# Scaling a gathered row in two halves, so that the adding engine can begin on the first

## The chip, the cores and the metric

The kernel runs on one core of one Trainium2 chip. The metric is device time in microseconds (us), the median of the runs shown. Five engines work side by side and meet only at semaphores: TensorE (PE in the profile, with its weight loads as PEld), VectorE (DVE), ScalarE (ACT), GpSimd (POOL) and SyncE (SP). Transfers run on 16 DMA engines.

## The reference, cut to what matters

The program is one layer of a transformer over 1024 tokens of width 1024. Its last part, and the longest, is PEER: each token looks up 128 of 16384 single-neuron experts (8 heads, 16 each) and adds their value rows, weighted.

```python
def block(args):
    xb, eb, gb = args
    ub = u[eb]
    act = jax.nn.gelu(jnp.einsum('thkd,td->thk', ub, xb).astype(jnp.float32),
                      approximate=False)
    w = (gb * act).astype(xb.dtype)
    return jnp.einsum('thk,thkd->td', w, v_emb[eb])
```

For a block of 128 tokens, u[eb] and v_emb[eb] are 128 gathered rows for each token. The kernel keeps u and v side by side in one table `uv`, so one gathered row holds 2048 numbers.

## The kernel before, in words

The phases ahead (norm, gated linear attention, most of the stick-breaking attention, memory attention for the first half of the tokens) end some 740 us into the span. Then `expert_phase` runs to the end. Its main loop goes over 8 blocks of 128 tokens, in each over 8 heads, in each over 16 chosen experts: 1024 steps, numbered R. A step treats one "row": for each of the 128 tokens (one to a partition) the 8 KB of its R-th expert, 1 MB in all.

Rows pass through a ring of 8 buffers (`Ring`: `early_rows` and `rows`, four each). The way of row R:

1. POOL waits until row R-8 has been used (`row_used`) and issues the indirect gather (line 2029).
2. DVE waits for it to land and takes the product of its u half with the tokens, summed (line 3045, `dots`).
3. ACT waits for `dots`, applies Gelu to the 128x1 result (line 3223), multiplies by the gate (line 3225), and scales the v half, 128x1024, in place by this weight (line 3231), which counts up `row_scaled`. The weight is an operand with one number for each partition.
4. PE waits for `row_scaled` and adds the v half to the block's sum `expert_acc` in PSUM with 8 transposing products of 128x128 (line 3539). The eighth counts up `row_used`, which frees the buffer.

The last three rows (LAST) end differently: the first of them is scaled as the others and added by DVE (line 2694) with the last two, which DVE scales itself.

Around these steps each engine has side work, put into the stream at fixed values of R by the tables `Later` and `Dense` through the functions `later(R)` and `densely(R)`: the rest of the layer for the second half of the tokens (attention, memory attention, query and key products), the choice of experts for coming groups, and from R about 524 a dense treatment of the 16 most wanted experts' tiles for the last three blocks, whose rows are then not gathered (their index lies out of bounds, in the list `expert_sk`). Every engine takes its stream in order. On ACT the side work lies between line 3231 of one row and line 3223 of the next; twice in a group of 16 rows ACT changes its function table.

Of the kernel before, what the change touches and what calls it, by code (L numbers as in the profile page):

```python
# [12 lines left out]
ACT = mybir.ActivationFunctionType  # L13
# [8 lines left out]
HALF = 512  # L22
# [43 lines left out]
class Core:  # L66
# [53 lines left out]
    def sb(self, name, shape, dt=F32, ctx=None, side=None):  # L120
        return (ctx or self.ctx).enter_context(self.nc.sbuf_tensor(name, shape, dt, side=side))
# [2209 lines left out]
def expert_phase(co, choice, ring, scores, rstd, uv, gf, g_final, out, k_t, v_m, z_b, mix_b, w_out, w_mq, w_mo, w_pq,  # L2331
# [3 lines left out]
    nc = co.nc  # L2335
# [48 lines left out]
    with ExitStack() as cx:  # L2384
# [8 lines left out]
        wt = sb("wt", [P, 2, 2, TOPK])  # L2393
# [95 lines left out]
        def rows_of(g):  # L2489

            b, h = divmod(g - PH * dense.FIRST, PH)
            if b < 0:
                return places_of(g)
            cols = slice(TOPK * h, TOPK * (h + 1))
            return skip_index[:, b, cols], skip_gates[:, b, cols]

        def position(g):

            return g if g < PH * HB else dense.turn_of[g]
# [165 lines left out]
        def _(dve):  # L2665
# [19 lines left out]
            def row_sum(R):  # L2685

                first = NB * BLOCK - LAST
                v = rows[R % ROWS][:, D:E]
                before = rows[first % ROWS][:, D:E]
                last = R == NB * BLOCK - 1  # L2690
                r = R % TOPK
                dve.wait_ge(row_scaled, first + 1)
                dve.wait_ge(last_weighed, R - first)
                return nc.vector.scalar_tensor_tensor(hb[:, :] if last else before, v, wt[:, (PH - 1) % 2, 1, r:r + 1], before,
                                                      ALU.mult, ALU.add)
# [379 lines left out]
        def _(act):  # L3075
            link = Chain(act, act_done)

            def scores_in(n):
                g = dense.group.get(n, n)
                dst = s_in[:, n % 2, :, :]  # L3080
                if at.EARLY // 2 <= g < PH:
                    act.wait_ge(a_kept, 2 * (g - at.EARLY // 2 + 1))
                if g >= PH * HB:
                    act.wait_ge(side_kept, 4 * (g % PH + 1))
                dst = dst.rearrange("p c n -> p (c n)")
                nc.scalar.activation(dst, group_scores(g), ACT.Copy).then_inc(s_ready, 1)

            def sum_squares(b):
                act.wait_ge(acc_turned, b + 1)
                nc.scalar.activation(hb[:, :], accs[b % 2][:, :], ACT.Square, accum_out=small2[:, 0:1]).then_inc(summed, 1)  # L3090

            def finish(b):
                act.preload_act_table_set(LN_EXP)
                act.wait_ge(var_ready, b + 1)
                link(nc.scalar.activation(small2[:, 2:3], small2[:, 1:2], ACT.Ln))
                nc.scalar.activation(small2[:, 3:4], small2[:, 2:3], ACT.Exp, scale=-0.5).then_inc(guess_ready, 1)
# [105 lines left out]
            def body(b, odd, more, last):  # L3202
                for h in range(PH):
                    g, s = PH * b + h, h % 2
                    _, row_gate = rows_of(g)
                    link.restart()
                    if g < PH * dense.FIRST:
                        act.wait_ge(gate_ready, position(g) + 1)
                    else:
                        act.wait_ge(skipped, (g - PH * dense.FIRST) // 2 + 1)  # L3210
                    for r in range(TOPK):
                        if r == (15 if g + AHEAD + 1 < PH else 13) and g + AHEAD + 1 < PH * HB:

                            act.wait_ge(index_ready, g + AHEAD)
                            scores_in(g + AHEAD + 1)
                        if r == 12 and g + AHEAD < PH * HB:
                            choice.exps(act, g + AHEAD, best_ready, exp_ready)
                        if r == 4 and h == 0 and 0 < b <= dense.FIRST:
                            sum_squares(b - 1)
                        if r == 8 and h == 0 and 0 < b <= dense.FIRST:  # L3220
                            finish(b - 1)
                        act.wait_ge(dots, TOPK * g + r + 1)
                        link(nc.scalar.activation(wt[:, s, 0, r:r + 1], dot[:, s, r:r + 1], ACT.Gelu))  # L3223
                        R = TOPK * g + r
                        link(nc.scalar.activation(wt[:, s, 1, r:r + 1], wt[:, s, 0, r:r + 1], ACT.Copy,  # L3225
                                                  scale=row_gate[:, r:r + 1]))
                        if R > NB * BLOCK - LAST:
                            act.sem_inc(last_weighed, 1)
                            continue
                        v = rows[R % ROWS][:, D:E]  # L3230
                        nc.scalar.activation(v, v, ACT.Copy, scale=wt[:, s, 1, r:r + 1]).then_inc(row_scaled, 1)  # L3231
                        later(R)
                        if R == NB * BLOCK - LAST:
                            act.wait_ge(row_used, R)
                            nc.scalar.activation(acc_sb[:, :, :], accs[odd][:, :].rearrange("p (k t) -> p k t", t=P),
                                                 ACT.Copy).then_inc(acc_kept, 1)

            act.sem_inc(s_ready, AHEAD)
            act.sem_inc(exp_ready, AHEAD)
            scores_in(AHEAD)  # L3240
            over_blocks(act, body)
            act.preload_act_table_set(LN_EXP)
            act.wait_ge(last_summed, 1)
# [6 lines left out]
        def _(pe):  # L3250
# [143 lines left out]
            def inject(b, acc, begins):  # L3394

                for k in range(KT):
                    nc.tensor.matmul(acc[:, k * P:(k + 1) * P], co.H[:, b, k * P:(k + 1) * P], co.ident[:, :],
                                     start=begins and k % 4 == 0, stop=False, is_transpose=True, skip_group_check=True)
# [116 lines left out]
            def turn_back(b, acc):  # L3515

                pe.wait_ge(acc_kept, b + 1)
                for k in range(KT):
                    last = nc.tensor.matmul(acc[:, k * P:(k + 1) * P], acc_sb[:, k, :], co.ident[:, :], start=k % 4 == 0,
                                            stop=k % 4 == 3, is_transpose=True, skip_group_check=True)  # L3520
                last.then_inc(acc_turned, 1)

            def body(b, odd, more, last):
                acc = accs[odd]
                if b == 1:
                    pe.wait_ge(a_kept, at.LATE)
                if b >= dense.FIRST + 2:
                    pe.wait_ge(rows_added, b - dense.FIRST - 1)
                elif b >= 2:
                    pe.wait_ge(out_ready, b - 1)  # L3530
                if b >= dense.FIRST:
                    pe.wait_ge(skipped, PH // 2 * (b - dense.FIRST + 1))
                else:
                    inject(b, acc, True)
                for r in range(BLOCK - LAST if last else BLOCK):
                    R = BLOCK * b + r
                    pe.wait_ge(row_scaled, R + 1)
                    for k in range(KT):
                        last_mm = nc.tensor.matmul(acc[:, k * P:(k + 1) * P], rows[R % ROWS][:, D + k * P:D + (k + 1) * P],  # L3539
                                                   co.ident[:, :], start=b >= dense.FIRST and r == 0 and k % 4 == 0, stop=False,  # L3540
                                                   is_transpose=True, skip_group_check=True)
                    last_mm.then_inc(row_used, 1)
                    if r == 1 and more:
                        turn_back(b - 1, accs[1 - odd])
                    later(R)

            over_blocks(pe, body)
            turn_back(NB - 1, accs[(NB - 1) % 2])
    co.end_phase()
# [202 lines left out]
```

## Time and profile before

| what | value |
|---|---|
| median of 3 runs | 3348.26 us (3347.88 to 3351.38) |
| the profiled execution, its own time | 3351.4 us |
| its span | 3349.7 us |
| mean granted clock of TensorE | 0.914 |
| PE, PEld busy | 2730.9 us (82%), 2067.2 us (62%) |
| DVE busy | 2386.9 us (71%) |
| ACT busy | 2272.8 us (68%) |
| POOL busy | 1388.5 us (41%) |

Busy times are sums over the whole span, in which phases with quite different limits follow each other. What is asked of an engine is therefore read from stretches of the span.

### The profile page before, as it was taken

What the parts mean: (1) busy time and instruction counts of PE and PEld (TensorE: products, weight loads), DVE (VectorE), ACT (ScalarE), POOL (GpSimd) and SP (SyncE); (2) the same over time, 40 slices, a digit from 0 to 9 for tenths busy, and PEclk for the clock granted to TensorE, in tenths of its full rate; (3) what the DMA queues carried; (4) which work ended last, traced back from release to release, by engine and by line L of the source; (5) the groups of instructions that cost most, each with busy time, mean ns of one, the idle gap of its engine ahead of it and who ended that gap; (6) DMA issues with size and microseconds to landing.
All of it is one profiled execution on the core that took longest, in us unless ns stands there. A gap on an engine that the chain in (4) does not pass through costs nothing.

```text
span 3349.7 us, 47831 instructions
## 1 busy us (share of the span) xinstructions
PE 2730.9 (82%) x16625; PEld 2067.2 (62%) x16625; DVE 2386.9 (71%) x5661; ACT 2272.8 (68%) x4096; POOL 1388.5 (41%) x1158
## 2 busy tenths in 40 slices
PE   8999989889987887787778677776688878878985
PEld 6777667765665664554665454555566658767654
DVE  5554445466788985676776667899988899877556
ACT  3222553236778886786987777767888886887777
POOL 0000100034544553444544443445456654566764
PEclk9999999999999899889789889998899987897997
DMA  3001143149999999999999999999999998999998
GB/s 115 25 33 38 64 139 126 63 164 408 417 418 420 411 415 420 420 414 420 418 407 420 420 415 420 411 418 398 419 365 384 372 359 306 348 400 390 407 399 321
DMA packets 198354, 1099.19 MB, mean 328 GB/s; under 512 B 33767, under 2 KB 49415, under 8 KB 77704
## 3 DMA queue, kind: packets, MB, share of 16 engines
q0 software_dynamic: 152064, 1001.19, 74.0%
q1 hardware_dynamic: 46050, 94.97, 7.9%
q8 instruction: 130, 2.13, 0.3%
q14 instruction: 110, 0.90, 0.1%
HBM read 1173.94 MB, written 11.54 MB: 354 GB/s over the span
## 4 chain that ended last, share of the span: by engine, by line
DMA 24%; DVE 16%; PE 15%; ACT 14%; issue 7%; POOL 2%; DVEq 0%; POOLq 0%; ACTq 0%
DMA early_rows<-in_uv,choice_index 12%; PE expert_acc L3539 7%; DVE scores L3045 5%; DMA rows<-in_uv,expert_sk 3%; ACT early_rows L3231 3%; DMA early_rows<-in_uv,expert_sk 3%; ACT rows L3231 3%; DMA rows<-in_uv,choice_index 2%; DMA rows<-in_uv,scores 2%; DVE early_rows L3045 2%; ACT expert_wt L3225 2%; ACT L3223 2%; DMA early_rows<-in_uv,scores 1%; ACT L1920 1%; ACT expert_wt L3223 1%
## 5 line engine op out<-in xcount | busy, mean ns | idle before, releaser
L3539 PE MATMUL expert_acc<-ident,rows 128*128 128x128 f32 x4072 | 622.1, 305 | 277.7 <-ACT rows L3231 276.2
L3539 PEld LDWEIGHTS expert_acc<-ident,rows 128*128 128x128 f32 x4072 | 524.5, 158 | 471.7 <-ACT rows L3231 421.5
L3539 PE MATMUL expert_acc<-ident,early_rows 128*128 128x128 f32 x4096 | 601.7, 297 | 238.2 <-ACT early_rows L3231 235.8
L3539 PEld LDWEIGHTS expert_acc<-ident,early_rows 128*128 128x128 f32 x4096 | 503.9, 153 | 440.1 <-ACT early_rows L3231 389.4
L3231 ACT ACTIVATE early_rows<-early_rows,expert_wt 128x1024 f32<-128x1024 f32 x512 | 588.6, 1150 | 16.7
L3231 ACT ACTIVATE rows<-rows,expert_wt 128x1024 f32<-128x1024 f32 x510 | 586.2, 1149 | 16.6
L3223 ACT ACTIVATE expert_wt<-expert_dot 128x1 f32<-128x1 f32 x1024 | 202.5, 198 | 484.4 <-DVE expert_dot L3045 479.9
L2029 POOL DMA_INDIRECT rows<-in_uv,choice_index x256 | 317.7, 1241 | 397.1 <-PE expert_acc L3539 353.1
L2029 POOL DMA_INDIRECT early_rows<-in_uv,choice_index x256 | 321.7, 1257 | 338.7 <-PE expert_acc L3539 293.8
L3045 DVE CUSTOM_DVE_ANT_0 rows<-rows,expert_xn 128x1024 f32<-128x1024 f32 x256 | 312.9, 1222 | 149.2 <-DMA rows<-in_uv,choice_index 148.5
L3045 DVE CUSTOM_DVE_ANT_0 early_rows<-early_rows,expert_xn 128x1024 f32<-128x1024 f32 x256 | 312.8, 1222 | 124.1 <-DMA early_rows<-in_uv,choice_index 122.0
L3045 DVE CUSTOM_DVE_ANT_0 scores<-rows,expert_xn 128x1024 f32<-128x1024 f32 x256 | 313.2, 1224 | 104.1 <-DMA rows<-in_uv,expert_sk 83.2
L3045 DVE CUSTOM_DVE_ANT_0 scores<-early_rows,expert_xn 128x1024 f32<-128x1024 f32 x256 | 313.2, 1223 | 79.5 <-DMA early_rows<-in_uv,expert_sk 65.5
L2029 POOL DMA_INDIRECT early_rows<-in_uv,expert_sk x192 | 255.0, 1328 | 170.4 <-PE expert_acc L3539 124.6
L2029 POOL DMA_INDIRECT rows<-in_uv,expert_sk x192 | 247.8, 1291 | 168.3 <-PE expert_acc L3539 119.3
L3225 ACT ACTIVATE expert_wt<-expert_wt,choice_gate 128x1 f32<-128x1 f32 x512 | 150.7, 294 | 16.6
L3280 PE MATMUL expert_side<-z_b,expert_w_raw 128*128 128x512 f32 x256 | 137.0, 618 | 0.0
L3265 PE MATMUL expert_side<-expert_w_raw,mix_b 128*128 128x512 f32 x256 | 129.9, 617 | 0.0
L3225 ACT ACTIVATE expert_wt<-expert_wt,expert_row_gates 128x1 f32<-128x1 f32 x384 | 113.1, 295 | 12.5
L2029 POOL DMA_INDIRECT rows<-in_uv,scores x64 | 81.8, 1278 | 94.2 <-PE expert_acc L3539 84.3
L2029 POOL DMA_INDIRECT early_rows<-in_uv,scores x64 | 79.7, 1245 | 83.1 <-PE expert_acc L3539 73.2
L2063 POOL IOTA choice_iota<- 128x16 f32 x1 | 0.1, 139 | 259.6 <-issue 259.6
(518 smaller groups left out, 5112.9 us busy)
## 6 DMA issues: line engine op xcount, KB each, us to landing
H<-in_x SPq DMA_DIRECT2D x8, 1024.0 KB, 10.7
expert_w_raw<-in_w_pq SPq DMA_DIRECT2D x16, 512.0 KB, 10.9
stick_w_raw<-in_w_feat SPq DMA_DIRECT2D x8, 512.0 KB, 3.4
tok_w_raw<-in_w_tok SPq DMA_DIRECT2D x8, 512.0 KB, 3.3
out_w_raw<-in_w_out SPq DMA_DIRECT2D x8, 512.0 KB, 3.5
mkv_w_raw<-in_w_mk SPq DMA_DIRECT2D x16, 256.0 KB, 4.0
mkv_w_raw<-in_w_mv SPq DMA_DIRECT2D x16, 256.0 KB, 3.0
pq_w_raw<-in_w_mq SPq DMA_DIRECT2D x8, 512.0 KB, 3.4
```

Of the source, the lines that this page charges most:

```text
L1920: self.nc.scalar.activation(self.best[:, q, :], self.best[:, q, :], ACT.Exp, bias=self.small[:, 0, q:q + 1], accum_out=self.small[:, 1, q: ...
L2029: pool.indirect_dma_start(out=self.rows[R % self.ROWS], out_offset=None, in_=uv, in_offset=bass.IndirectOffsetOnAxis(ap=index, axis=0), bo ...
L2063: pool.iota(choice.iota[:, :], pattern=[[1, TOPK]], base=0, channel_multiplier=0, allow_small_or_imprecise_dtypes=True).then_inc(iota_read ...
L3045: nc.vector.tensor_tensor_reduce(u if b < HB else junk, u, xn[:, :], 1.0, 0.0, ALU.mult, ALU.add, dot[:, h % 2, r:r + 1]).then_inc(dots, 1)
L3223: link(nc.scalar.activation(wt[:, s, 0, r:r + 1], dot[:, s, r:r + 1], ACT.Gelu))
L3225: link(nc.scalar.activation(wt[:, s, 1, r:r + 1], wt[:, s, 0, r:r + 1], ACT.Copy, scale=row_gate[:, r:r + 1]))
L3231: nc.scalar.activation(v, v, ACT.Copy, scale=wt[:, s, 1, r:r + 1]).then_inc(row_scaled, 1)
L3265: last = nc.tensor.matmul(side[j], mix_b[:, k, j * P:(j + 1) * P], w_raw[:, slot, :], start=k == 0, stop=k == KT - 1)
L3280: last = nc.tensor.matmul(side[n % 2], w_raw[:, slot, j * P:(j + 1) * P], x, start=k == 0, stop=k == KT - 1)
L3539: last_mm = nc.tensor.matmul(acc[:, k * P:(k + 1) * P], rows[R % ROWS][:, D + k * P:D + (k + 1) * P], co.ident[:, :], start=b >= dense.FIR ...
```

## The change

ACT scales the v half of each row with two instructions of 128x512 where it was one of 128x1024, and each counts up `row_scaled`. PE waits before the first product of a row for the first half, and before the fifth for the second half. DVE's wait for the first of the last three rows is adapted to the doubled count. What is computed is the same.

```diff
@@ row_sum
-                dve.wait_ge(row_scaled, first + 1)
+                dve.wait_ge(row_scaled, 2 * (first + 1))
@@ ScalarE, body
                         v = rows[R % ROWS][:, D:E]
-                        nc.scalar.activation(v, v, ACT.Copy, scale=wt[:, s, 1, r:r + 1]).then_inc(row_scaled, 1)
+                        for part in range(2):
+                            half_row = v[:, part * HALF:(part + 1) * HALF]
+                            nc.scalar.activation(half_row, half_row, ACT.Copy, scale=wt[:, s, 1, r:r + 1]).then_inc(row_scaled, 1)
                         later(R)
@@ TensorE, body
-                    pe.wait_ge(row_scaled, R + 1)
                     for k in range(KT):
+                        if k % 4 == 0:
+                            pe.wait_ge(row_scaled, 2 * R + k // 4 + 1)
                         last_mm = nc.tensor.matmul(acc[:, k * P:(k + 1) * P], rows[R % ROWS][:, D + k * P:D + (k + 1) * P],
                                                    co.ident[:, :], start=b >= dense.FIRST and r == 0 and k % 4 == 0, stop=False,
                                                    is_transpose=True, skip_group_check=True)
```

## Rows read from the trace of the kernel before

**Rows 1.** The page: busy share of the DMA engines in 40 slices of the span.
```profile
DMA  3001143149999999999999999999999998999998
```

**Rows 2.** Busy time of each engine in four stretches.
```profile
core 0: us, PE busy (x) PEld busy (x) DVE busy (x) ACT busy (x) POOL busy (x), PEclk, DMA share, GB/s
1600.00:1750.00 150.00, 107.67 (x696) 98.50 (x695) 113.53 (x294) 137.02 (x250) 74.47 (x60) 0.80 1.01 411
2400.00:2700.00 300.00, 249.16 (x1736) 186.08 (x1734) 258.81 (x701) 262.25 (x473) 180.88 (x139) 0.95 0.97 380
2700.00:2900.00 200.00, 155.31 (x1333) 140.76 (x1333) 182.64 (x477) 151.26 (x280) 101.78 (x80) 0.78 0.88 324
2900.00:3349.00 449.00, 364.82 (x2572) 287.52 (x2571) 302.19 (x527) 342.55 (x630) 276.40 (x213) 0.88 0.97 384
```

**Rows 3.** Gathers, median us to landing: 1500 to 1600, 2600 to 2700, 2800 to 2900.
```profile
early_rows<-in_uv,choice_index POOLq DMA_INDIRECT x20, 17.0
early_rows<-in_uv,expert_sk POOLq DMA_INDIRECT x24, 9.5
early_rows<-in_uv,expert_sk POOLq DMA_INDIRECT x21, 8.1
```

**Rows 4.** Groups by shape on ACT: count, busy us, mean ns, idle before.
```profile
L3231 ACT ACTIVATE early_rows<-early_rows,expert_wt 128x1024 f32<-128x1024 f32 x512 | 588.6, 1150 | 16.7
L3231 ACT ACTIVATE rows<-rows,expert_wt 128x1024 f32<-128x1024 f32 x510 | 586.2, 1149 | 16.6
L3225 ACT ACTIVATE expert_wt<-expert_wt,choice_gate 128x1 f32<-128x1 f32 x512 | 150.7, 294 | 16.6
```

**Rows 5.** Timeline of ACT, two pairs of neighbours: start us, us.
```profile
466.65 1.06 ACT L158 ACTIVATE out_w_hi<-out_w_raw 128x1024 fp32r<-128x1024 f32 x1 [4.05 <-PE mixout_bank L171]
467.62 1.14 ACT L677 ACTIVATE memnorm_xs<-m_tok,rstd 128x1024 f32<-128x1024 f32 x1
...
2633.70 1.15 ACT L3231 ACTIVATE early_rows<-early_rows,expert_wt 128x1024 f32<-128x1024 f32 x1
2634.75 1.00 ACT L3111 ACTIVATE expert_qt<-expert_side 128x1024 f32<-128x1024 f32 x1
```

**Rows 6.** The chain that ended last: start us, us, what.
```profile
2415.12 1.15 ACT rows L3231
2416.29 1.28 ACT L1920
...
2420.15 1.16 ACT early_rows L3231
2421.35 1.53 PE expert_acc L3539 x8
...
2787.94 1.97 PE expert_acc L3539 x8
...
3240.40 1.16 ACT early_rows L3231
3241.61 1.09 PE expert_acc L3539 x8
...
3315.36 1.16 ACT early_rows L3231
3316.56 4.31 PE expert_acc L3539 x24
...
3334.88 1.15 ACT rows L3231
3336.03 0.91 ACT expert_hb L3235
```

**Rows 7.** Busy time of ACT in line 3231 alone, in three stretches.
```profile
1600.00:1750.00 150.00, 68.98 (x60) 0.80 1.01 411
2400.00:2700.00 300.00, 141.35 (x123) 0.95 0.97 380
2700.00:2900.00 200.00, 93.23 (x81) 0.78 0.88 324
```

**Rows 8.** Waits of ACT, 2400 to 2700: us in total, times, longest us.
```profile
ACT expert_wt L3223 <- DVE expert_dot L3045: 28.9, 44, 2.7
```

## The prediction

> **What bounds the kernel now.** I began with the slices of the page. From slice 9 of 40 (counted from 0; a slice is 84 us, so from about 750 us) to the end the DMA engines stand at 8 or 9 tenths or more [rows 1]. That is the gather of the expert rows. Then I cut this part by stretches [rows 2]. Three regimes are to be seen there:
>
> - Up to about 2400 us the DMA share is 1.01, even in 1600 to 1750, the stretch with the busiest ACT (137.0 of 150 us). The gathers set the pace. The time from issue to landing says how much reserve the ring has: 17.0 us there against 8.1 us where the DMA engines are not full (share 0.88 in 2700 to 2900) [rows 2, 3]. So some 17.0 - 8.1 = 9 us of that time is queueing, and a buffer freed earlier only waits longer in that queue, while one freed up to 9 us late does no harm.
> - From 2400 to 2700 us the share is 0.97, and ACT is the busiest engine: 262.3 of 300 us. The queueing is down to 9.5 - 8.1 = 1.4 us [rows 2, 3].
> - From 2700 to 2900 us the share is 0.88. DVE is busiest with 182.6 of 200 us, ACT has 151.3 [rows 2]. After 2900 us the mean share is 0.97 again.
>
> Last, the chain that ended last. After 2400 us ACT's scaling of a row stands in it and hands over to PE 27 times, from 2420.15 to 3315.36 us, and to another instruction of ACT 47 times, from 2415.12 to 3334.88 us [rows 6]. The first kind can gain by the change, the second can only lose. By stretches, the first kind comes 6, 4 and 17 times (2400 to 2700, to 2900, to the end), and the second 27, 6 and 14.
>
> **The edit on ACT.** One instruction of 1.15 us goes, two of half the length come. With one number for a column and the same kind of scale operand the instruction takes 294 ns [rows 4]. So an element costs (1150 - 294)/1023 = 0.837 ns and a half 294 + 511 x 0.837 = 722 ns. Neighbours overlap: the instruction behind line 3231 starts 2634.75 - 2633.70 = 1.05 us after it, 0.10 us before it ends; and one with a scale operand starts 467.62 - 466.65 = 0.97 us after a predecessor of 1.06 us, 0.09 us before that one's end [rows 5]. The second half thus starts at 0.72 - 0.10 = 0.62 us and ends at 0.62 + 0.72 = 1.34 us. ACT needs 1.34 - 1.15 = 0.19 us more for each row. Bounds: no such pair stands in the trace. If it doesn't overlap at all, 2 x 0.72 - 1.15 = 0.29 us; if the overlap is twice what these rows show, 0.10 us. Both pairs speak for 0.19, which I take.
>
> Over the 1022 rows that is 194 us of ACT's time. The work that hides it is the DMA queue, where it is full.
>
> The Trainium skill weighs just this in "Perfetto Trace Analysis", section "Optimizing Scalar/DVE Operations": breaking up an instruction can release waiting engines sooner if ScalarE isn't saturated, and if it is, larger operations are better, with about 93 ns of overhead for each one on SBUF. By that figure the extra cost would be, as an estimate, 0.09 us a row and 123 x 0.093 = 11 us in 2400 to 2700, half of what the rows give. The rows here carry the further cost of the scale operand, and the sum goes by them.
>
> **The edit on PE.** Before, with ACT starting at 0, PE starts at 1.20 us (3241.61 - 3240.40 = 1.21) and its 8 products take 1.09 us at the full clock and 1.97 at the half [rows 6], so the buffer is free at 2.29 or 3.17 us. After, the first half is ready at 0.72, PE starts at 0.77, and is through four products at 0.77 + 0.55 = 1.32; the second half is ready at 1.34, so products five to eight run from 1.39 to 1.94. That is 2.29 - 1.94 = 0.35 us sooner. At the half clock PE is through four at 1.76 and through eight at 2.74, 0.43 us sooner. This holds only where PE stood waiting. Where it has a backlog both halves are ready, and the second wait costs nothing. Where it comes in early it is held in the middle of a row for 0.02 to 0.05 us; behind it in its stream lie side products, and these come 0.35 us sooner too. The lower bound of the gain is 0, if ACT was late by 0.19 us a row for two rows before.
>
> The adapted wait on DVE costs nothing: it stands in the last 20 us, behind waits that last longer anyway.
>
> **The sum by stretches.**
>
> - Up to 2400 us: 0. In 1600 to 1750 ACT has 60 rows [rows 7], +11.4 us on 137.0, and between its dependent instructions 3 x 0.033 us a row lie idle (16.6 us over 512 in [rows 4]), 6 us. Together 154 of 150 us: ACT falls behind by some 4 us, which the 9 us of queueing take up. If that cover were gone, it would be 4 us here.
> - 2400 to 2700 us: ACT has 123 rows [rows 7]. 262.3 + 123 x 0.19 + 123 x 0.10 = 297.9 of 300 us. It waits for DVE's products 28.9 us now [rows 8]; to hold the pace it would have to give up nearly all of that, in 44 waits of at most 2.7 us that don't lie where the load does. Lower bound: only the links of the chain count, 27 x 0.19 = 5.1 us. Upper bound: every row, 123 x 0.19 = 23.4 us. I take 11, nearer to the lower since much of the waiting can be filled. From it go 6 hand-overs to PE at 0.35, 2 us. Result +9.
> - 2700 to 2900 us: 6 x 0.19 - 4 x 0.43 = -0.6 us. DVE goes on setting the pace: -1.
> - 2900 us to the end: 14 x 0.19 = +2.7, and 17 x 0.35 = -6.0 us, of which the DMA queue lets only a part through (share 0.97 [rows 2]); I take a third of the second, -2. Result +1.
>
> Sum: +9 - 1 + 1 = +9 us on the profiled execution's own 3351.4 us (span 3349.7, 1.7 us around it). That execution lies 3.1 us above the median of 3348.3, so the change is added to the median: 3357 us. A measurement of this kernel tells about 0.2%, 6.7 us, from no change.
>
> **The rivals.**
>
> A. *Faster by earlier release.* If ACT's lateness is taken up by its waits for DVE, what remains is each hand-over: 27 x 0.35 = 9.5 us, a bit more at the half clock, some of it lost again in ACT's own links (5.1 + 1.1 + 2.7 = 9 us at most). The place is 2400 to 3100 us, where the ring is nearly without reserve. For it: PE waits for line 3231, not for its own work. Against it: the DMA share is at 0.97 and more except in 200 us, and there DVE is the bound. It decides if a split costs ACT 0.10 us and not 0.19. Time: 3348 - 8 = 3340 us. Chance 0.18. The rule on breaking up instructions that the Trainium skill states in "Perfetto Trace Analysis" (section above) gives this case if ACT doesn't count as saturated.
>
> B. *Hidden anyway.* The gathers set the pace nearly everywhere, and the small loss and gain after 2400 us cancel (the links of the chain alone: +9 on ACT, -2 - 2 - 6 on PE). Time 3348 us. Chance 0.20.
>
> C. *ACT becomes the bound.* Every row from 2400 to 2900 us exposes its cost, (123 + 81) x 0.19 = 39 us, and the 4 us of 1600 to 1750 come through since the reserve is less than the landing times make it look. For it: ACT's sum of 298 in 300 us. Against it: in 2700 to 2900 ACT has 151 + 81 x 0.29 = 175 of 200 us. Up to 3348 + 43 - 8 = 3383 us; its middle 3375. Chance 0.14.
>
> The forecast, a small loss between 2400 and 2700 us, has 0.48.
>
> **How the numbers follow.** The forecast's own range is 3350 to 3368: lower end by the chain's links in 2400 to 2700 (5.1 - 2, less 1), upper end by most of its rows (23 - 2). About two thirds of it, 0.31, lie above 3355. Slower by over 0.2%: 0.31 + 0.14 = 0.45. Within 0.2%: 0.17 + 0.18 of B = 0.35. Faster: 0.18 and 0.02 of B = 0.20. The range, 3341 to 3376, leaves out about half of A and half of C, and reaches to the other cases on both sides.
>
> **What the profile after would show.** Line 3231 has 2044 instructions of 128x512, of about 0.72 us, the second 0.62 us after the first (0.53 would be the bound of 0.10, 0.72 that of 0.29). PE's first product of a waiting row starts 0.77 us after ACT's first half and its last ends near 1.94. Up to 2400 us the DMA share stays at 1.01, and the landing time in 1500 to 1600 falls from 17.0 by some us. In 2400 to 2700 ACT's busy time rises to more than 90% with fewer rows than 123, its wait for DVE falls below 15 us, and the DMA share falls below 0.97. If the share there stays or rises, the forecast is wrong and A or B holds; if rows lie further apart already in 1600 to 1750, C.

## The result and the profile after

| | before | after |
|---|---|---|
| median of 20 runs | 3348.64 us | 3353.16 us |
| lowest to highest | 3341.45 to 3352.75 | 3348.89 to 3357.93 |
| profiled execution, its span | 3349.7 us | 3348.5 us |
| ACT busy | 2272.8 us | 2449.2 us |

The ratio is 1.0013, with a 95% interval of 1.0007 to 1.0019: 4.4 us slower (2.3 to 6.4), less than the 0.2% that were to count as a difference, but the interval lies wholly above 1. The forecast was 3357 us, in a range of 3341 to 3376.

The two profiled executions don't show it: the span after is even 1.2 us shorter. The reason lies ahead of the changed part, where nothing was changed. DVE's first instruction of block 0 (line 3026) starts at 740.4 us before and at 736.5 after. From there to the end it is 2609.3 us before and 2612.0 after. So all that follows is counted from block to block.

The page after, busy times with counts, the slices of ACT and of the DMA engines, and the groups of the scaling and the adding (line 3231 is now 3233, and 3539 is 3542):

```profile
PE 2787.6 (83%) x16625; PEld 2042.1 (61%) x16625; DVE 2387.4 (71%) x5661; ACT 2449.2 (73%) x5118; POOL 1394.6 (42%) x1158
ACT  3222553237888996887997877778899987898878
DMA  3001243149999999999999999999999998899998
L3542 PE MATMUL expert_acc<-ident,rows 128*128 128x128 f32 x4072 | 657.1, 306 | 257.5 <-ACT rows L3233 254.9
L3542 PE MATMUL expert_acc<-ident,early_rows 128*128 128x128 f32 x4096 | 637.5, 298 | 194.1 <-ACT early_rows L3233 191.6
L3233 ACT ACTIVATE early_rows<-early_rows,expert_wt 128x512 f32<-128x512 f32 x1024 | 684.0, 715 | 16.7
L3233 ACT ACTIVATE rows<-rows,expert_wt 128x512 f32<-128x512 f32 x1020 | 681.2, 715 | 16.6
```

A half takes 715 ns (forecast 722). ACT is busy with the scaling for 684.0 + 681.2 = 1365.2 us where it was 1174.8 [rows 4]: 190.4 us over 1022 rows, 0.186 us a row, against 0.19 in the forecast. The second figure of interest is how soon PE is through. The timeline of ACT and PE after, in a place where PE waited (start us, us):

```profile
3322.38 1.33 ACT L3233 ACTIVATE rows<-rows,expert_wt 128x512 f32<-128x512 f32 x2
3323.15 0.42 PEld L3542 LDWEIGHTS expert_acc<-ident,rows 128*128 128x128 f32 x4 [0.76 <-ACT rows L3233]
3323.16 1.27 PE L3542 MATMUL expert_acc<-ident,rows 128*128 128x128 f32 x8 [0.52 <-ACT rows L3233]
3323.77 0.42 PEld L3542 LDWEIGHTS expert_acc<-ident,rows 128*128 128x128 f32 x4 [0.20 <-ACT rows L3233]
```

PE starts 3323.16 - 3322.38 = 0.78 us after ACT (forecast 0.77), and the loads for the second half 1.39 us after it (1.39). But it ends at 0.78 + 1.27 = 2.05 us, not at 1.94: four products that start anew take 2.05 - 1.39 = 0.66 us, not half of the 1.09 of eight in one go. The release comes 2.29 - 2.05 = 0.24 us sooner, two thirds of the 0.35 us that were counted on. Where PE runs at its half clock (granted 0.50 here), the second half is ready before the first four products are through, and all eight go in one go as before:

```profile
2808.00 1.33 ACT L3233 ACTIVATE early_rows<-early_rows,expert_wt 128x512 f32<-128x512 f32 x2
2808.77 1.97 PE L3542 MATMUL expert_acc<-ident,early_rows 128*128 128x128 f32 x8 [0.67 <-ACT early_rows L3233]
```

There PE ends at 0.77 + 1.97 = 2.74 us, which is 3.17 - 2.74 = 0.43 us sooner, as forecast.

Busy times by stretch, after, to be set beside [rows 2], and ACT's wait for DVE in 2400 to 2700, beside [rows 8]:

```profile
1600.00:1750.00 150.00, 107.38 (x687) 93.62 (x688) 113.47 (x293) 144.71 (x307) 71.17 (x59) 0.85 1.00 406
2400.00:2700.00 300.00, 254.13 (x1722) 180.63 (x1721) 256.95 (x695) 280.09 (x592) 186.80 (x138) 0.97 0.97 376
2700.00:2900.00 200.00, 158.55 (x1333) 138.34 (x1334) 182.62 (x477) 166.03 (x363) 105.44 (x80) 0.80 0.88 324
2900.00:3349.00 449.00, 373.88 (x2571) 279.71 (x2570) 302.45 (x529) 377.19 (x831) 284.82 (x213) 0.90 0.96 384
```

```profile
ACT expert_wt L3223 <- DVE expert_dot L3045: 10.3, 17, 2.5
```

In 2400 to 2700 ACT is busy 280.1 us where it was 262.3, and its wait for DVE fell from 28.9 to 10.3 us: what was added was taken from waiting. The gathers moved 376 GB/s there, 380 before.

Of the signs that the prediction named, three came (halves of 0.72 us, ACT over 90% busy in 2400 to 2700, its wait for DVE below 15 us). Two did not. The landing time of `early_rows` in 1500 to 1600 didn't fall by some us: it is 17.6 us (17.0 in the second profile of the change). And the DMA share in 2400 to 2700, which was to fall below 0.97 or else the forecast was wrong, reads 0.97 again (0.96 in the second profile). To two digits this sign decides nothing; the GB/s, 380 and 381 in two profiles before, 376 and 374 after, do fall. The scaled rows in that stretch are 122 to 123, not clearly fewer. Rows further apart in 1600 to 1750 were to be the sign of C; there are 59 and 58 in the two profiles after, where two before have 60 and 61, so a little of it is there.

### The profile page after: what moved, and what is told of

The parts are those of the page before. It is cut to its first block, busy times and chain, and to the rows that moved or that the text cites. A ratio compares the mean times of both kernels' runs of the same rounds, so it can differ in the third digit from the quotient of the medians.

```text
span 3348.5 us, 48853 instructions
## 1 busy us (share of the span) xinstructions
PE 2787.6 (83%) x16625; PEld 2042.1 (61%) x16625; DVE 2387.4 (71%) x5661; ACT 2449.2 (73%) x5118; POOL 1394.6 (42%) x1158
## 4 chain that ended last, share of the span: by engine, by line
DMA 25%; ACT 15%; DVE 15%; PE 13%; issue 7%; POOL 2%; POOLq 0%; DVEq 0%; ACTq 0%
DMA early_rows<-in_uv,choice_index 11%; PE expert_acc L3542 7%; DVE scores L3045 5%; DMA rows<-in_uv,choice_index 4%; ACT early_rows L3233 4%; ACT rows L3233 3%; DMA rows<-in_uv,expert_sk 3%; DMA early_rows<-in_uv,expert_sk 2%; ACT expert_wt L3225 2%; DMA early_rows<-in_uv,scores 2%; DMA rows<-in_uv,scores 2%; DVE early_rows L3045 2%; ACT L3223 2%; ACT expert_wt L3223 1%; ACT L1920 1%
## 5 line engine op out<-in xcount | busy, mean ns | idle before, releaser
L3542 PE MATMUL expert_acc<-ident,rows 128*128 128x128 f32 x4072 | 657.1, 306 | 257.5 <-ACT rows L3233 254.9
L3542 PEld LDWEIGHTS expert_acc<-ident,rows 128*128 128x128 f32 x4072 | 512.4, 156 | 493.5 <-ACT rows L3233 443.8
L3542 PE MATMUL expert_acc<-ident,early_rows 128*128 128x128 f32 x4096 | 637.5, 298 | 194.1 <-ACT early_rows L3233 191.6
L3542 PEld LDWEIGHTS expert_acc<-ident,early_rows 128*128 128x128 f32 x4096 | 495.1, 151 | 434.2 <-ACT early_rows L3233 388.8
L3233 ACT ACTIVATE early_rows<-early_rows,expert_wt 128x512 f32<-128x512 f32 x1024 | 684.0, 715 | 16.7
L3233 ACT ACTIVATE rows<-rows,expert_wt 128x512 f32<-128x512 f32 x1020 | 681.2, 715 | 16.6
L2029 POOL DMA_INDIRECT rows<-in_uv,expert_sk x192 | 254.9, 1328 | 159.0 <-PE expert_acc L3542 107.3
```

The lines of the kernel that those rows point to most:

```text
L2029: pool.indirect_dma_start(out=self.rows[R % self.ROWS], out_offset=None, in_=uv, in_offset=bass.IndirectOffsetOnAxis(ap=index, axis=0), bo ...
L3233: nc.scalar.activation(half_row, half_row, ACT.Copy, scale=wt[:, s, 1, r:r + 1]).then_inc(row_scaled, 1)
```

## The experiments

Medians stand beside the kernel before in the same series: 3350.09 us for experiments 1 to 4, 3349.56 for 5 to 8, 3349.97 for 9 to 11. The differences in us are those of the ratio and of its 95% interval, times 3349.

**1. Halves, but one wait.** ACT as in the change, PE waits for both halves before its first product.

```diff
-                        if k % 4 == 0:
-                            pe.wait_ge(row_scaled, 2 * R + k // 4 + 1)
+                        if k == 0:
+                            pe.wait_ge(row_scaled, 2 * R + 2)
```

> The row is scaled in two halves, but TensorE waits for both before its first product, so ScalarE's cost of the split stands alone and a buffer comes free 0.19 us later than before instead of 0.35 us sooner. Theory 1 (the split costs by ScalarE's extra time, and the earlier release gives a part of it back): slower than the changed kernel, +8 to +14 us on the kernel before against the +4.5 us of the change. Theory 2 (the release gives nothing, since the gathers or the dot products set the pace): the same +4 to +5 us as the change. Theory 3 (ScalarE's time is hidden too, and the +4.5 us come from TensorE's wait in the middle of a row): 0 to +2 us.

Measured: 3366.63 us, ratio 1.0057 (1.0042 to 1.0073), +19 us (14 to 24). Theories 2 and 3 are out, and even the first had it too small: the early start of PE, which is all that this kernel lacks, is worth 19 - 4 = 15 us, give or take some 5. In its profile PE, where it waited, is through 2.48 us after ACT's start (3338.34 to 3339.73, and 1.09 us of products), 0.19 us later than before.

**2. ACT's time alone.** The kernel before with one small instruction of ACT behind every row; its result goes into a tile that nothing reads.

```diff
                         nc.scalar.activation(v, v, ACT.Copy, scale=wt[:, s, 1, r:r + 1]).then_inc(row_scaled, 1)
+                        nc.scalar.activation(extra[:, 0:1], wt[:, s, 1, r:r + 1], ACT.Copy, scale=wt[:, s, 1, r:r + 1])
```

> The row is scaled by one instruction as before, and ScalarE gets one more 128x1 instruction behind it, with a scale operand, in every row (0.29 us long, some 0.19 us of start to start). The release of a row is as before; only ScalarE's time grows by as much as in the change. Theory 1: slower by some +6 to +12 us, more than the change (no earlier release to set against it) and less than the halves with one wait. Theory 2 (no gain from the release): +4 to +5 us. Theory 3: 0 to +2 us.

Measured: 3362.39 us, ratio 1.0039 (1.0023 to 1.0054), +13 us (8 to 18); just above the expectation, in the order it gave. ACT is busy 2449.0 us in this kernel and 2449.2 with the change, so the added time is the same. So the change is a sum of two larger terms: +13 us for ACT's time, and -9 us for PE being through sooner, by 0.24 us where it waited at the full clock. The first experiment agrees in the order: through 0.19 us later instead, it stands 6 us above this one, though the two intervals overlap. All three lie near a line of 3 to 4 us for 0.1 us. Two ways for the gain are not told apart: when PE is through sooner, the buffer is free sooner and PE's side products come sooner too. No run separates them.

Where do the 13 us arise? About 7 of them before 1766 us, in blocks 0 to 2. The sums over that part, first of this kernel, then of the one before (columns as in [rows 2]):

```profile
740.00:1766.00 1026.00, 822.65 (x4645) 605.66 (x4646) 755.34 (x1847) 860.24 (x1802) 487.12 (x384) 0.90 1.00 410
```

```profile
740.00:1766.00 1026.00, 817.89 (x4679) 599.94 (x4680) 763.18 (x1861) 803.69 (x1439) 489.71 (x388) 0.91 1.01 414
```

The share reads 1.00 after 1.01, and the bytes moved fell from 414 to 410 GB/s: 1%, of 1026 us. Slices of 25 us are too fine to place the loss by one profile: with the extra time seven of the 41 from 750 us have a share below 0.995, in two profiles of the kernel before one and three, in two of the change two and six.

The stretch with the busiest ACT, 1600 to 1750, tells more. The prediction reckoned there with 9 us of queueing, from the 17.0 us to landing of the gathers issued in 1500 to 1600. Its own gathers, and ACT's wait for DVE in it, before:

```profile
early_rows<-in_uv,choice_index POOLq DMA_INDIRECT x28, 11.2
ACT expert_wt L3223 <- DVE expert_dot L3045: 2.9, 5, 0.8
```

So by the prediction's own measure only 11.2 - 8.1 = 3.1 us of queueing are left in this stretch, less than the 4 us that ACT was to fall behind. With the extra time the landing is down to

```profile
early_rows<-in_uv,choice_index POOLq DMA_INDIRECT x28, 10.1
```

and ACT waits for DVE no more; block 2, in which the stretch lies, is 339.5 us long, where it was 335.2 and 334.4 in two profiles before.

**3 and 4. Halves in some of the blocks.** The choice is made by a function of R; whole rows elsewhere. Shown is experiment 3; experiment 4 has `R < 5 * BLOCK`. ACT's loop and DVE's wait follow the same function.

```diff
+    def parts_of(R):
+
+        return 2 if R >= 5 * BLOCK else 1
+
+    scaled_before = [0]
+    for R in range(NB * BLOCK):
+        scaled_before.append(scaled_before[-1] + parts_of(R))
...
-                        if k % 4 == 0:
-                            pe.wait_ge(row_scaled, 2 * R + k // 4 + 1)
+                        if k % (KT // parts_of(R)) == 0:
+                            pe.wait_ge(row_scaled, scaled_before[R] + k * parts_of(R) // KT + 1)
```

> Halves only in blocks 5, 6 and 7 (from about 2458 us), whole rows before. Theory 1, as predicted (before 2400 us the queue of the gathers hides all of it): +4 to +6 us, that of the whole change. Rival (the cost lies where ScalarE is busiest in blocks 1 and 2, and the last blocks gain as much as they lose): -2 to +2 us.

> Halves only in blocks 0 to 4 (740 to about 2458 us), whole rows after. Theory 1, as predicted: -1 to +1 us. Rival (the reserve of the ring is smaller than the landing times make it look, and ScalarE falls behind in blocks 1 and 2): +3 to +5 us, most of the change.

Measured: 3354.43 us in the last three blocks, ratio 1.0013 (1.0002 to 1.0023), +4.4 us (0.7 to 7.7); 3350.63 us in the first five, ratio 0.9998 (0.9989 to 1.0007), -0.7 us (-3.7 to 2.3). As expected for both: the loss comes mostly or wholly from the last three.

**5. Halves in block 7 alone.** As above, with `R >= 7 * BLOCK`.

> Halves only in block 7 (the last 128 rows, from about 3049 us). In one profile each, block 7 took 300.9 us before and 296.1 us after the change, and blocks 5 and 6 together 5.2 us more. Theory 1 (in block 7 ScalarE has time to spare, and the earlier release of the buffers counts): -1 to -4 us on the kernel before. Rival (the gathers set the pace there, their share is 0.99 to 1.01; the difference was scatter): within 1 us.

Measured: 3346.31 us, ratio 0.9993 (0.9983 to 1.0003), -2.3 us (-5.7 to 1.0). The interval holds 0, so it doesn't tell the two apart.

**6. The cost twice.** The changed kernel with the small instruction of experiment 2 behind the second half.

> The changed kernel with one more 128x1 instruction of ScalarE behind every row, some 0.19 us of start to start: the suspected cost twice, the early release kept. Extra time alone measured +13.8 us on the kernel before. Theory 1 (ScalarE's time is the cost, and it grows faster than in proportion as ScalarE runs out of spare time): +22 to +40 us on the kernel before, so 18 or more on the change. Rival (the cost of the change lies in TensorE's middle wait or in noise, and ScalarE's time counts only linearly): +17 to +19 us.

Measured: 3393.68 us, ratio 1.0129 (1.0113 to 1.0145), +43 us (38 to 49, four executions): 39 on the change. This is the first theory, just above its range of 22 to 40 us, for an addition that cost 13 where ACT had more time to spare. ACT's waits in 2400 to 2700, and the gathers, in that kernel:

```profile
ACT expert_wt L3224 <- DVE expert_dot L3046: 3.3, 4, 1.6
```

```profile
2400.00:2700.00 300.00, 251.65 (x1662) 179.32 (x1661) 248.28 (x677) 288.63 (x687) 164.51 (x132) 0.93 0.94 365
```

Hardly anything is left to take: 28.9, 10.3, 3.3 us of waiting, and 380, 376, 365 GB/s.

**7. Halves, but not near the table loads.** In blocks 5 and 6 the rows around ACT's function for the choice of experts stay whole.

```diff
-        return 2 if R >= 5 * BLOCK else 1
+        if R < 5 * BLOCK:
+            return 1
+        return 1 if any(E - 6 <= R <= E + 4 for E in dense.exps) else 2
```

> Halves in block 7, and in blocks 5 and 6 only in the rows that don't lie within 6 rows ahead of or 4 behind ScalarE's function for the choice of experts with its two table loads (65 of 128 rows in block 5, 105 in block 6); whole rows in blocks 0 to 4. Theory 1 (the cost arises where ScalarE's rows lead to that function in the chain, the gain where TensorE waits): -1 to -5 us. Rival (ScalarE's lateness carries over more rows than that): +1 to +4 us, as with halves in all of the last three blocks.

Measured: 3350.28 us, ratio 1.0000 (0.9991 to 1.0010), 0 us (-3.0 to 3.4). The median is in neither expectation and the interval reaches into both: by the time alone it can't be told from the kernel before, nor from experiment 3. Block 5 is 298.6 us long, as with whole rows, which speaks for the loss being gone.

**8 and 11. Both kernels profiled again.**

> The kernel before, unchanged, profiled once more: how much the length of one block of 128 rows scatters from profile to profile. If by 1 us or less, the differences of 2 to 5 us between blocks of the two profiles are the change's; if by 3 us, they are not.

> The changed kernel, profiled once more, for the scatter of the blocks: if the loss of the change is real and sits in block 5, that block takes 301 to 303 us again (298 to 299 with whole rows), and blocks 0 to 4 stay within 1 to 3 us of the kernel before.

One execution each, 3348.04 and 3357.63 us, taken for the lengths of the blocks. By the first expectation, the differences of single blocks are the change's only where one kernel scatters by 1 us or so. The two profiles of the kernel before differ by 1.1 us in block 5, but by 3.2 in block 1, 2.9 in block 6 and 5.6 in block 7, so of single blocks only block 5 and block 2 (0.8 us apart) are read here. The second expectation holds for block 5, 303.2 us, and fails for blocks 0 to 4: they take 1723.7 us together, 3.3 and 6.1 more than before, where 1 to 3 were expected.

**9. Halves in block 5 alone.** `5 * BLOCK <= R < 6 * BLOCK`.

> Halves only in block 5 (rows 640 to 767, some 2458 to 2757 us), where five profiles of whole rows and four of halves differ by about 3 us. Theory 1 (the loss of the change sits in this block, where ScalarE had 28.9 us of waiting left): +2.5 to +4 us on the kernel before, the block itself 301 to 303 us long. Rival (the loss is spread over the blocks and this one only shifts it): within 1.5 us, with a longer block 5 and a shorter block 6.

Measured: 3353.80 us, ratio 1.0007 (0.9996 to 1.0019), +2.3 us (-1.3 to 6.4); by the time alone not clear of 0, and between the two expectations. Its block 5 is 303.4 us long, and its block 6 isn't shorter (293.7 us, after 291.5 and 294.4 before), so the loss isn't merely shifted.

**10. As 7, in all blocks.** The rows around r = 12 of each group in blocks 0 to 3 are left whole too.

```diff
+        busy = [TOPK * g + 12 for g in range(PH * HB - AHEAD)] + list(dense.exps)
+        return 1 if any(E - 6 <= R <= E + 4 for E in busy) else 2
```

> Halves in all blocks, but not in the rows that lie within 6 ahead of or 4 behind ScalarE's function for the choice of experts (40 to 52 rows of 128 are halved in blocks 0 to 4, then 65, 105 and 128). Extra ScalarE time cost blocks 0 to 2 some 9 us, and the halves gave all of it back there. Theory 1 (the halves gain where TensorE waits, in blocks 0 to 2 too, once the loaded rows are left whole): -2 to -6 us. Rival (in blocks 0 to 4 the gathers hide what is gained): -1 to +1 us, as the version with whole rows there.

Measured: 3349.33 us, ratio 0.9994 (0.9983 to 1.0005), -2.0 us (-5.7 to 1.7). It can't be told from experiment 7 nor from the kernel before.

**The blocks, over all profiles.** DVE starts a block with line 3026, so a block's length is the distance of two such starts. Blocks 0 to 2, 3 and 4, 5, and 6 and 7 (to the end of the span), in us:

| kernel | 0 to 2 | 3, 4 | 5 | 6, 7 |
|---|---|---|---|---|
| before, two profiles | 1025.4, 1027.8 | 692.2, 692.6 | 299.3, 298.2 | 592.4, 589.6 |
| change, two profiles | 1029.4, 1032.9 | 690.5, 690.8 | 301.4, 303.2 | 590.7, 590.4 |
| 1 halves, one wait | 1037.2 | 690.2 | 303.5 | 595.3 |
| 2 extra ACT time | 1034.1 | 690.2 | 303.2 | 592.4 |
| 3 halves in 5 to 7 | 1026.8 | 692.0 | 302.4 | 591.2 |
| 4 halves in 0 to 4 | 1027.1 | 690.8 | 302.6 | 591.1 |
| 5 halves in 7 | 1024.9 | 692.1 | 298.5 | 591.3 |
| 6 the cost twice | 1045.0 | 690.3 | 311.5 | 600.5 |
| 7 away from loads, 5 to 7 | 1025.1 | 692.1 | 298.6 | 592.7 |
| 9 halves in 5 | 1025.6 | 691.6 | 303.4 | 590.3 |
| 10 away from loads, all | 1027.1 | 693.4 | 297.5 | 591.2 |

The scatter of one kernel is 0.3 to 3.5 us in a cell. Two things stand out.

- Block 5 takes 301.4 to 303.5 us in the five profiles in which all its rows are halved (the change twice, experiments 1, 3 and 9). Whole rows give 298.2 to 299.3 in three (before twice, experiment 5), and halves in only 65 of its 128 rows 297.5 and 298.6 (experiments 7 and 10). Whole rows with the extra time give 303.2 (one profile): ACT's time alone makes the block as long. One profile doesn't fit: experiment 4 has whole rows there and 302.6, and I can't say why.
- Blocks 0 to 2 take 1034.1 and 1037.2 us with extra time of ACT and no earlier release, and 1024.9 to 1027.8 in six profiles with whole rows there. With halves and the earlier release they lie between, at 1027.1, 1029.4 and 1032.9.

The starts of blocks 5 and 6 in the two profiles with which the study began, before and after:

```profile
2458.02 1.28 DVE L3026 SCALAR_TENSOR_TENSOR expert_xn<-H,rstd,gffn 128x1024 f32<-128x1024 f32 x1
2757.29 1.28 DVE L3026 SCALAR_TENSOR_TENSOR expert_xn<-H,rstd,gffn 128x1024 f32<-128x1024 f32 x1
```

```profile
2456.40 1.28 DVE L3026 SCALAR_TENSOR_TENSOR expert_xn<-H,rstd,gffn 128x1024 f32<-128x1024 f32 x1
2757.79 1.28 DVE L3026 SCALAR_TENSOR_TENSOR expert_xn<-H,rstd,gffn 128x1024 f32<-128x1024 f32 x1
```

## Why the prediction was right, and where only its sum was

- **ACT's extra time a row**: forecast 0.19 us, measured 0.186. Right. The Trainium skill ("ScalarE: Activation LUTs", section "What ACT_TABLE_LOAD costs") gives the same by its own figures, as an estimate: 279 ns + 512 x 0.833 ns for an instruction with one operand a partition, less 93 ns where neighbours overlap, so 1.32 us for the pair; the trace has 1.33.
- **The earlier release**: at the full clock 0.35 us forecast, 0.24 measured. The term was mis-sized, since half of the eight products' time was taken for four products. A burst of four that starts anew takes 0.66 us, not 0.55. At the half clock 0.43 us, as forecast.
- **What the release is worth**: forecast at 2 us in 2400 to 2700, some 4 after that and nothing before, from 27 hand-overs in the chain. Measured 9 us for 0.24 us (experiment 2 against the change) and 15 for 0.43 (experiment 1 against the change), each give or take some 5. The hand-overs of one chain counted too few. That a later release also makes other links late is my reading; no run shows it.
- **"Up to 2400 us: 0"**: right as a result (experiment 4: -0.7 us), by luck. The step said that 9 us of queueing, read from 17.0 against 8.1 us to landing, hide ACT's 0.19 us a row. It took the reserve from 1500 to 1600 for the stretch behind it, where the landing time leaves 3.1 us. With the release unchanged the extra time made blocks 0 to 2 longer by some 7 us (1034.1 against 1025.4 and 1027.8). With the earlier release added it comes out near 0 up to 2400 us, so two terms that the sum had both at nothing there pay for each other. How nearly is open: the second profile of the change has 1032.9 in blocks 0 to 2.
- **"2400 to 2700 us: +9"**: the place is right, and the mechanism, ACT running out of waiting time, is shown by the extra time (28.9, 10.3, 3.3 us) and by the growth from 13 to 39 us for the same addition. The size was twice too large: the last three blocks lose 4.4 us (experiment 3), block 5 alone 2.3 by the time and about 4 by its length.
- **After 2700 us: 0** as forecast, within some us; experiment 5 leaves open whether block 7 gains 2 us.
- **The sum**: over all stretches the prediction put ACT's time at 11 + 1.1 + 2.7 = 15 us and the release at 2 + 1.7 + 2 = 6. Measured are 13 and 9, so +4.4 us where +9 was forecast. The two terms and their signs are right; that the totals come so near is in part luck, since half of the 13 us arise in blocks 0 to 2, where the sum had none.
- **The rivals**: A fails, with the 0.10 us that it needed. B's number, no change, lies as near to the result as the forecast does, but little is hidden: two terms of 13 and 9 us stand against each other. C is what the doubled cost brings (+43 us).

The Trainium skill's two rules on breaking up instructions ("Perfetto Trace Analysis", section "Optimizing Scalar/DVE Operations") are both seen here, in one kernel: PE, which had waited, is through sooner, and ACT, with little waiting left, pays. The runs put 9 and 13 us beside them.

## What to carry to other kernels

To cut an instruction in two so that the next engine can start is a trade: the fixed part of one more instruction, 0.19 us here, against the part of the latency that is really saved, 0.24 us here and not the half that it looks like. Measure both terms by themselves (both halves with one wait; the extra time with no halves): a result near zero can be a sum of two larger numbers, and the next addition to the same engine can cost more than the first (here 39 us after 13). A DMA share that reads 1.0 over a long stretch doesn't show that nothing else matters in it; look at the GB/s. And read the reserve, here the landing time, in the very stretch for which it is counted on.

## What the runs showed that I had not expected

- The DMA share over 740 to 1766 us read 1.00 after 1.01 while the gathers slowed by 1% (414 to 410 GB/s). As a measure of reserve it is blunt near 1.
- The part of the program that is the same in all kernels scatters: block 0 began between 736.2 and 741.7 us. That is more than the change, and a single pair of spans had the wrong sign.
- Blocks 3 and 4 are some 1.6 us shorter where every row of blocks 0 to 4 costs ACT more (690.2 to 690.8 in six profiles, 691.6 to 692.6 in six with whole rows there). Experiment 10, with halves in a part of those rows, has 693.4. It was not followed up.
